# Mixing attention: biased scores and their running minimum in one VectorE instruction, from negated scaled queries

## The chip, the cores and the metric

One core of a Trainium2 chip runs the whole model: two transformer layers with a mixing sublayer each, then a recurrent layer and a stick-breaking layer. The metric is the device time of one execution in microseconds (us), less is better. Five engines work side by side, each through its own queue in order: TensorE (PE in the profile; PEld are its weight loads), VectorE (DVE), ScalarE (ACT), GpSimd (POOL) and SyncE (SP). They wait for each other through semaphores.

## The reference, cut to what matters

The change touches the two attentions of the mixing sublayer. Six heads attend in a neighbourhood (NA) with a bias table and a column mask, six in a window of 128 tokens (SWA) with a learned sink. Both also attend to 256 context tokens. Per query block:

```
s_lat = einsum(q, k_lat) * scale + bias          # SWA: no bias
s_lat = where(valid, s_lat, -1e30)
s_ctx = einsum(q, k_ctx) * scale
p = softmax(concatenate([s_lat, s_ctx]))         # SWA: the sink is one more column
o = einsum(p_lat, v_lat) + einsum(p_ctx, v_ctx)
```

## The kernel before, in words

The sublayer `mix` first projects queries, keys and values; VectorE copies the query and key tiles out of PSUM into `QK` (L1609 to L1613). Then attention runs as a list of steps (`att_steps`). A step is one pair of heads (`x` = 0, 1) and one block `t` of 128 queries. Six groups of steps (`ot` = 0 to 5: three NA, three SWA) follow each other. In layer 0 a group has six steps: four latent ones (`t` = 0 to 3, with `w` = 256, 384, 384, 256 latent keys and 256 context keys) and two that see the 256 context keys alone. In layer 1 a group has the four latent steps. So layer 0 has 36 steps, layer 1 has 24.

Every step passes through three in-order queues. The score tile `SB` has three buffers, the softmax statistics `SM` two.

- PE, for loop index `i`: `scores(i+1)` (latent matmuls L2412 into PSUM banks 0 and 1, then context matmuls L2415 into banks 2 and 3), `values(i-2)` (L2450, probabilities by values), `transposes(i-1)` (L2424). `scores` waits until banks 0 to 3 of the step before have been read.
- DVE: for step `i+1` the instruction at L1686 reads the latent scores of both heads from PSUM, multiplies by the scale, adds the bias and writes `SB`; L1690 takes the maximum over all columns of both heads; L1691 negates it. Then for step `i`: reciprocal of the row sums (L1696) and two scalings of the probabilities (L1699). At a group's end it copies the output out (L1706, L1708, L1710) and makes a low part (L1262). At an NA group's start it adds the column mask to the bias table (L1670). A sink column is copied at L1680.
- ACT: for step `i+1` a scaled copy of the context scores from PSUM to `SB` (L990); then for step `i` an exponential for each head with the row sum accumulated (L998); then for step `i-1` the copies of the transposed probabilities from PSUM (L1011, L1014); at a group's end the high part of the output (L713).

So a step's scores go PE, then DVE (latent) and ACT (context), back to DVE for the maximum, ACT for the exponentials, DVE for the scaling, PE for the transposes, ACT for the copies, PE for the values. After attention, the output projection (L2227) begins; its matmuls then fill PE without gaps. The names of semaphores that matter: `s_mm` (score matmuls done), `s_lat` (L1686 done), `s_ctx` (L990 done), `s_max` (maximum ready).

Of the kernel before, what the change touches and what calls it, by code (L numbers as in the profile page):

```python
# [21 lines left out]
P = 128  # L22
# [123 lines left out]
def build(nc, xT, ctxT, metaT, const, masks, condb, condc, modw, wu, wg, rpb, rope, four, four_c, gatew, kept, out, stop=99):  # L146
# [54 lines left out]
    MASKS = place("att_masks", [P, 7 * NA_C + 384], F32, a_t + 20480)  # L201
    RT = place("rope_tmp", [P, 2, SEQ], F32, a_t)
# [123 lines left out]
    s_lat, s_out, vf_ready, vf_rows = sem("score_bias"), sem("pv_read"), sem("v_features_ready"), sem("v_rows_mm")  # L326
# [214 lines left out]
    with nc.Block() as block:  # L541
# [155 lines left out]
        def _(act):  # L697
# [253 lines left out]
            def mix(sub, b):  # L951
# [31 lines left out]
                for i in range(-1, N + 2):  # L983
                    if i + 1 < N:
                        st, a = steps[i + 1], a0 + i + 1
                        w = st["w"]
                        act.wait_ge(s_mm, a + 1)
                        if i >= 2:
                            act.wait_ge(s_tr, tr0 + steps[i - 1]["tr0"])
                        act.activation(SB[:, a % 3, :, 1 + w:1 + w + CTX], row2(PSF[:, 2 * SEQ:4 * SEQ])[:, :, 0:CTX], ACT.Copy,  # L990
                                       scale=QSCALE).then_inc(s_ctx, 1)
                    if 0 <= i < N:
# [3 lines left out]
                        act.wait_ge(s_max, a + 1)  # L996
                        for x in range(2):
                            ins = act.activation(SB[:, a % 3, x, lo:1 + w], SB[:, a % 3, x, lo:1 + w], ACT.Exp,  # L998
                                                 bias=SM[:, a % 2, 1, x:x + 1], accum_out=SM[:, a % 2, 2, x:x + 1])
                        ins.then_inc(s_exp, 1)  # L1000
                        if st["ot"] == 1 and st["t"] == 0:
                            act.wait_ge(s_lat, 24 * mx + 4)
                            bias_load(2)
# [246 lines left out]
        def _(dve):  # L1250
# [349 lines left out]
            def mix(sub, b):  # L1600
# [3 lines left out]
                for j in range(10):  # L1604
# [3 lines left out]
                    if j < 6:  # L1608
                        ins = dve.tensor_copy(column_tiles(QK[:, j, 0:SEQ]), by_column(ps[:, 0:SEQ]))  # L1609
                        if Tj > SEQ:  # L1610
                            ins = dve.tensor_copy(QK[:, j, SEQ:T1], ps[:, SEQ:T1])
# [50 lines left out]
                for i in range(-1, N + 3):  # L1662
                    if i + 1 < N:
                        st, a = steps[i + 1], a0 + i + 1
                        sb, w, ot = SB[:, a % 3], st["w"], st["ot"]
                        if st["na"] and st["t"] == 0:
                            dve.wait_ge(tb_in[ot % 2], 16 * (mx + 1 if ot == 1 else 2 * mx + 1 + ot // 2))
                            for x in range(2):
                                tbh = TB[:, ot % 2, x].rearrange("p (n r c) -> p n r c", n=7, r=8)
                                ins = dve.tensor_tensor(tbh, tbh, MASKS[:, 0:7 * NA_C].rearrange("p (n c) -> p n c", n=7).unsqueeze(2)  # L1670
                                                        .broadcast_to([P, 7, 8, NA_C]), ALU.add)
# [4 lines left out]
                        lo = 1  # L1676
                        if st["sink"] is not None:
                            lo = 0
# [1257 lines left out]
```

## Time and profile before

| | us |
|---|---|
| median of three runs | 3761.63 (3756.4 to 3768.09) |
| span of the profiled execution, first to last instruction | 3755.4 |
| attention of layer 0 (first bias addition to first L2227) | 783.28 to 928.27: 144.99 |
| attention of layer 1 | 2253.16 to 2364.69: 111.53 |
| PE busy over the span | 3530.5 (94%) |
| DVE busy over the span | 2183.8 (58%) |
| ACT busy over the span | 1434.2 (38%) |

The profile gives no own run time of the profiled execution; its span lies 1.0 us under the fastest of the three runs and 6.2 us under their median. Busy shares over the whole span are averages over stages with different limits; PE is nearly full in the matrix stages and far less so in the two attention stages.

### The profile page before, as it was taken

How to read it: one execution, taken by the hardware profiler on the slowest of the kernel's cores; microseconds unless marked ns; L12 is line 12 of the kernel's file. 1: busy time of each engine (PE TensorE's matmuls, PEld its weight loads, DVE VectorE, ACT ScalarE, POOL GpSimd, SP SyncE). 2: the span in 40 equal slices, each digit the busy share in tenths (PEclk: the TensorE clock that was granted, in tenths of full speed). 3: DMA queues.
4: the chain of work that ended last, by engine and by line, in shares of the span. 5: the costliest groups of instructions: out<-in, count | busy, mean ns of one | idle time of the engine just before them, and what ended most of it. 6: DMA issues, size and time to landing. Idle time of an engine off the chain costs nothing.

```text
span 3755.4 us, 52062 instructions
## 1 busy us (share of the span) xinstructions
PE 3530.5 (94%) x19855; PEld 3030.4 (81%) x19855; DVE 2183.8 (58%) x3395; ACT 1434.2 (38%) x2510; POOL 721.5 (19%) x299
## 2 busy tenths in 40 slices
PE   6899999988999999999999898899998999899998
PEld 4899997856789999789999676788878898589656
DVE  6888875167488888788887429421226462541134
ACT  4433333157353333543334317432234423221353
POOL 1111112200211111211111220244442232034202
PEclk9999999999999999999999998999998999799899
DMA  6333332110233332433333220123332222022101
GB/s 227 107 124 123 124 120 86 62 36 1 91 118 116 121 117 97 157 109 116 113 113 119 82 70 17 46 90 100 96 95 68 62 79 68 1 73 90 62 1 56
DMA packets 94531, 333.55 MB, mean 89 GB/s; under 512 B 12272, under 2 KB 14576, under 8 KB 93424
## 3 DMA queue, kind: packets, MB, share of 16 engines
q1 hardware_dynamic: 91248, 316.28, 25.5%
q10 hardware_dynamic: 3072, 14.40, 1.0%
q8 instruction: 140, 2.29, 0.2%
q14 instruction: 71, 0.58, 0.0%
HBM read 322.12 MB, written 8.52 MB: 88 GB/s over the span
## 4 chain that ended last, share of the span: by engine, by line
PE 60%; issue 23%; POOL 6%; DVE 6%; ACT 3%; DMA 2%; SPq 0%; POOLq 0%; DVEq 0%; ACTq 0%
PE psum L2348 21%; PE psum L2227 14%; PE psum L2207 13%; POOL w_parts L668 6%; PE psum L2652 1%; PE psum L2668 1%; PE psum L2262 1%; PE psum L2677 1%; PE psum L2450 1%; PE psum L2121 1%; DMA mod_ring<-modw_dram 1%; PE psum L2424 1%; DVE normed L1302 1%; PE psum L2556 1%; DVE mod_products L1390 0%
## 5 line engine op out<-in xcount | busy, mean ns | idle before, releaser
L668 POOL TENSOR_TENSOR w_parts<-w_raw,w_parts 128x1024 fp32r<-128x1024 f32 x289 | 702.5, 2432 | 2929.2 <-ACT w_parts L708 2916.8
L2207 PE MATMUL psum<-h_parts,w_parts 128*128 128x264 f32 (+1 forms) x5712 | 958.2, 330 | 46.8 <-issue 11.8
L2207 PEld LDWEIGHTS psum<-h_parts,w_parts 128*128 128x128 f32 x5712 | 855.4, 191 | 144.4 <-issue 44.6
L708 ACT ACTIVATE w_parts<-w_raw 128x1024 fp32r<-128x1024 f32 x283 | 300.1, 1061 | 1123.7 <-PE psum L2207 722.5
L2227 PE MATMUL psum<-w_parts,hidden_parts 128*128 128x512 f32 x2904 | 668.3, 391 | 16.5 <-DVE hidden_parts L1262 9.6
L2227 PEld LDWEIGHTS psum<-w_parts,hidden_parts 128*128 128x128 f32 x2904 | 544.6, 188 | 135.6 <-issue 14.6
L2348 PE MATMUL psum<-h_parts,w_parts 128*128 128x384 f32 x2880 | 531.6, 336 | 16.4 <-ACT y_tok L855 14.1
L2348 PEld LDWEIGHTS psum<-h_parts,w_parts 128*128 128x128 f32 x2880 | 505.4, 189 | 20.0 <-issue 17.0
L874 ACT ACTIVATE w_parts<-psum 128x512 fp32r<-128x512 f32 x240 | 143.7, 599 | 367.9 <-PE psum L2348 147.9
L2348 PE MATMUL psum<-h_sums,w_parts 128*128 128x384 f32 x1440 | 268.9, 334 | 0.0
L2348 PEld LDWEIGHTS psum<-h_sums,w_parts 128*128 128x128 f32 x1440 | 251.3, 188 | 0.0
L1390 DVE SCALAR_TENSOR_TENSOR mod_products<-mod_ring,cond_rows 128x1024 bf16<-128x1024 f32 x128 | 180.4, 1409 | 54.4 <-DMA mod_ring<-modw_dram 51.6
L1390 DVE SCALAR_TENSOR_TENSOR mod_ring<-mod_ring,cond_rows 128x1024 f32<-128x1024 f32 x128 | 202.0, 1578 | 0.0
L1358 DVE TENSOR_TENSOR y_tok<-y_tok,psum 128x512 f32<-128x512 f32 (+1 forms) x196 | 126.7, 682 | 122.6 <-PE psum L2227 121.2
L874 ACT ACTIVATE w_parts<-w_raw_pairs 128x512 fp32r<-128x512 f32 x180 | 113.5, 631 | 220.5 <-PE psum L2348 125.4
L1543 DVE TENSOR_TENSOR w_parts<-psum,w_parts 128x512 fp32r<-128x512 f32 x240 | 164.7, 686 | 20.7 <-ACT w_parts L874 19.8
L1543 DVE TENSOR_TENSOR w_parts<-w_raw_pairs,w_parts 128x512 fp32r<-128x512 f32 x180 | 123.9, 688 | 57.6 <-ACT w_parts L874 56.6
L2348 PE MATMUL psum<-h_sum,w_parts 128*128 128x384 f32 x720 | 134.9, 335 | 0.0
L2348 PEld LDWEIGHTS psum<-h_sum,w_parts 128*128 128x128 f32 x720 | 126.4, 189 | 0.0
L2227 PE MATMUL psum<-w_parts,h_parts 128*128 128x512 f32 x480 | 109.3, 389 | 2.3 <-DVE primer L1715 2.3
L1981 DVE SCALAR_TENSOR_TENSOR sb_softplus<-psum,sb_softplus 128x512 f32<-128x512 f32 (+2 forms) x48 | 27.8, 608 | 143.6 <-ACT sb_softplus L1183 143.6
L2172 PE MATMUL psum<-h_parts,w_parts 128*128 128x256 f32 (+1 forms) x528 | 103.7, 352 | 5.8 <-DVE h_parts L1294 5.5
(352 smaller groups left out, 4121.1 us busy)
## 6 DMA issues: line engine op xcount, KB each, us to landing
w_raw<-wu_dram SPq DMA_DIRECT2D x295, 512.0 KB, 3.6
mod_ring<-modw_dram SPq DMA_DIRECT2D x128, 512.0 KB, 4.4
w_raw_pairs<-wg_dram SPq DMA_DIRECT2D x120, 512.0 KB, 3.7
kept_dram<-resid SPq DMA_DIRECT2D x2, 3136.0 KB, 9.9
resid<-kept_dram SPq DMA_DIRECT2D x16, 392.0 KB, 5.8
na_bias<-rpb_dram ACTq DMA_DIRECT2D x6, 896.0 KB, 4.7
four_dft<-four_dram ACTq DMA_DIRECT2D x2, 2048.0 KB, 8.1
mod_first_k<-modw_dram SPq DMA_DIRECT2D x7, 512.0 KB, 10.0
```

The costliest lines, as they stand in the source:

```text
L668: pool.tensor_tensor(SPL[:, s % 2, 1], RAW[:, s % 2], SPL[:, s % 2, 0].bitcast(F32), ALU.subtract).then_inc(w_split, 1)
L708: act.activation(SPL[:, u % 2, 0], RAW[:, u % 2], ACT.Copy).then_inc(w_hi, 1)
L874: act.activation(w_block(n, 0), src, ACT.Copy).then_inc(block_hi, 1)
L1302: dve.scalar_tensor_tensor(normed_tile(sub, k, a, z), XT[:, k, META + a:META + z], mod_col(l, 3 * s + 1, k, int(a >= SEQ)), PS[:, 2, SEQ * ...
L1358: return dve.tensor_tensor(y, y, bank(t), ALU.add)
L1390: return dve.scalar_tensor_tensor(dst, MODW[:, d % 2], 1.0, CBC[:, c], ALU.mult, ALU.mult, accum_out=MODS[:, t, c:c + 1])
L1543: dve.tensor_tensor(w_block(n, 1), src, w_block(n, 0).bitcast(F32), ALU.subtract)\
L2121: ins = pe.matmul(PS[0:1, 2, SEQ * hi:SEQ * hi + z - a], col("ones"), SQE[:, m, a:z], start=m == 0, stop=m == DT - 1)
L2172: ins = pe.matmul(PS[:, (u + j) % 4, a:z], SPL[:, (u + j) % 2, wp, k], H[:, xp, k, a:z], start=k == 0 and n_ == 0, stop=k == DT - 1 and n_ ...
L2207: ins = pe.matmul(PS[:, pair, PSO[a]:PSO[a] + z - a], w[:, wp, k], src[:, xp, k, t0 + a:t0 + z], start=k == 0 and n_ == 0, stop=k == KT - ...
L2227: ins = pe.matmul(bank(t), src[:, xp, k, t * P:t * P + P], SPL[:, s, wp, 4 * c:4 * c + 4].rearrange("p k m -> p (k m)"), start=k == 0 and ...
L2348: ins = pe.matmul(bank(to, HT), w_block(n, wp)[:, k], moving(m, xp)[:, k], start=m in (1, 7, 2) and k == 0 and n_ == 0, stop=k == 3 and n_ ...
```

## The change

Queries are scaled and negated once, as they are copied out of PSUM (by -QSCALE), so PSUM holds negated scaled scores. Bias and masks change sign. VectorE then reads each head's scores from PSUM with one combined instruction (tensor_tensor_reduce) that adds a second operand (a column of zeros for context scores, bias or mask for latent ones), writes the sum to `SB`, and keeps the running minimum in one column of `SM`. The minimum of the context part (or of sink and context) is the starting value of the latent part. ScalarE's exponential takes scale -1. The maximum (L1690), the negation (L1691) and ScalarE's copy of the context scores (L990) go. The context matmuls stand ahead of the latent ones, and the latent ones wait by themselves. The core of the diff:

```diff
@@ ScalarE
-                for i in range(-1, N + 2):
-                    if i + 1 < N:
-                        st, a = steps[i + 1], a0 + i + 1
-                        w = st["w"]
-                        act.wait_ge(s_mm, a + 1)
-                        if i >= 2:
-                            act.wait_ge(s_tr, tr0 + steps[i - 1]["tr0"])
-                        act.activation(SB[:, a % 3, :, 1 + w:1 + w + CTX], row2(PSF[:, 2 * SEQ:4 * SEQ])[:, :, 0:CTX], ACT.Copy,
-                                       scale=QSCALE).then_inc(s_ctx, 1)
-                    if 0 <= i < N:
+                for i in range(N + 2):
+                    if i < N:
...
-                        act.wait_ge(s_max, a + 1)
                         for x in range(2):
-                            ins = act.activation(SB[:, a % 3, x, lo:1 + w], SB[:, a % 3, x, lo:1 + w], ACT.Exp,
+                            if st["lat"]:
+                                act.wait_ge(s_max, 2 * (24 * mx + st["nlat"]) + x + 1)
+                            else:
+                                act.wait_ge(s_ctx, 2 * a + x + 1)
+                            ins = act.activation(SB[:, a % 3, x, lo:1 + w], SB[:, a % 3, x, lo:1 + w], ACT.Exp, scale=-1.0,
                                                  bias=SM[:, a % 2, 1, x:x + 1], accum_out=SM[:, a % 2, 2, x:x + 1])
@@ VectorE, copies of queries (keys stay copies)
-                        ins = dve.tensor_copy(column_tiles(QK[:, j, 0:SEQ]), by_column(ps[:, 0:SEQ]))
+                    if j < 3:
+                        ins = dve.tensor_scalar(column_tiles(QK[:, j, 0:SEQ]), by_column(ps[:, 0:SEQ]), -QSCALE, None, ALU.mult)
...
@@ VectorE, a step's scores
-                            ins = dve.tensor_copy(sb[:, :, 0:1], sink[:, :, st["sink"]:st["sink"] + 1])
-                            if not st["lat"]:
-                                step(ins)
+                            step(dve.tensor_scalar(sb[:, :, 0:1], sink[:, :, st["sink"]:st["sink"] + 1], -1.0, None, ALU.mult))
+                        for x in range(2):
+                            least = SM[:, a % 2, 0 if st["lat"] else 1, x:x + 1]
+                            first = 3.0e38 if st["sink"] is None else sb[:, x, 0:1]
+                            dve.tensor_tensor_reduce(sb[:, x, 1 + w:1 + w + CTX], bank(2 + x, CTX), ZERO.broadcast_to([P, CTX]), 1.0, first,
+                                                     ALU.add, ALU.min, least).then_inc(s_ctx, 1)
                         if st["lat"]:
-                            dve.scalar_tensor_tensor(sb[:, :, 1:1 + w], PSF[:, 0:2 * SEQ].rearrange("p (x c) -> p x c", x=2)[:, :, 0:w],
-                                                     QSCALE, bias, ALU.mult, ALU.add).then_inc(s_lat, 1)
-                            dve.wait_ge(s_lat, 24 * mx + st["nlat"] + 1)
-                        dve.wait_ge(s_ctx, a + 1)
-                        step(dve.reduce_max(SM[:, a % 2, 0, :], sb[:, :, lo:1 + w + CTX], AX_X))
-                        dve.tensor_scalar(SM[:, a % 2, 1, :], SM[:, a % 2, 0, :], -1.0, None, ALU.mult).then_inc(s_max, 1)
+                            dve.wait_ge(s_mml, 24 * mx + st["nlat"] + 1)
+                            for x in range(2):
+                                dve.wait_ge(s_ctx, 2 * a + x + 1)
+                                bias = (TB[:, ot % 2, x, st["mask"]:st["mask"] + w] if st["na"] else MASKS[:, st["mask"]:st["mask"] + w])
+                                dve.tensor_tensor_reduce(sb[:, x, 1:1 + w], bank(x, w), bias, 1.0, SM[:, a % 2, 0, x:x + 1],
+                                                         ALU.add, ALU.min, SM[:, a % 2, 1, x:x + 1]).then_inc(s_max, 1)
@@ PE, scores(i)
                     if i >= 1:
-                        pe.wait_ge(s_lat, 24 * mx + st["nlat"])
-                        pe.wait_ge(s_ctx, a)
...
+                        pe.wait_ge(s_ctx, 2 * a)
                     for x in range(2):
                         rows = slice(x * HD, x * HD + HD)
                         ins = pe.matmul(bank(2 + x, CTX), QK[rows, st["q"], t:t + P],
                                         QK[rows, st["k"], SEQ:T1], start=True, stop=True)
                     ins.then_inc(s_mm, 1)
+                    if st["lat"]:
+                        if i >= 1:
+                            pe.wait_ge(s_max, 2 * (24 * mx + st["nlat"]))
+                        k0, k1 = st["lat"]
+                        for x in range(2):
...
+                        ins.then_inc(s_mml, 1)
```

On DVE, an SWA step of layer 0 with 384 latent keys stands like this before (`const` holds the sink, `att_masks` the mask; brackets name the semaphores waited for):

```order
L1680 COPY scores<-const 128x2 [waits prob_tr,score_mm,pv_read]
L1686 SCALAR_TENSOR_TENSOR scores<-psum,att_masks 128x2x384
L1690 TENSOR_REDUCE softmax_stats<-scores 128x2 [waits score_ctx,score_bias]
L1691 TENSOR_SCALAR softmax_stats<-softmax_stats 128x2 [waits dve_step]
L1696 RECIPROCAL softmax_stats<-softmax_stats 128x2 [waits score_exp]
```

And the next such step in the changed kernel (ISA is the combined instruction; the ISA row with 128x1 is its read of the minimum):

```order
L1679 TENSOR_SCALAR scores<-const 128x2 [waits prob_tr,score_mm]
L1683 ISA scores,softmax_stats<-psum,att_masks,scores 128x256 [waits dve_step]
L1683 ISA softmax_stats 128x1
L1683 ISA scores,softmax_stats<-psum,att_masks,scores 128x256
L1683 ISA softmax_stats 128x1
L1690 ISA scores,softmax_stats<-psum,att_masks,softmax_stats 128x384 [waits score_ctx,score_lat_mm]
L1690 ISA softmax_stats 128x1
L1690 ISA scores,softmax_stats<-psum,att_masks,softmax_stats 128x384 [waits score_ctx]
L1690 ISA softmax_stats 128x1
L1696 RECIPROCAL softmax_stats<-softmax_stats 128x2 [waits score_exp]
```

Three instructions over 768, 1282 and 2 columns per partition have become four over 256, 256, 384 and 384 with a read behind each; the wait for ScalarE's copy has become a wait for the latent matmuls, and the sink's instruction is now waited for.

On ACT, in an SWA group of layer 0, before:

```order
L990 ACTIVATE scores<-psum 128x2x256 [waits prob_tr,score_mm]
L998 ACTIVATE scores,softmax_stats<-scores,softmax_stats 128x641 [waits score_max]
L998 ACTIVATE scores,softmax_stats<-scores,softmax_stats 128x641
L1011 ACTIVATE probs_t<-psum 128x512 [waits prob_tr,pv_done]
L1011 ACTIVATE probs_t<-psum 128x512 [waits prob_tr]
```

and in the changed kernel:

```order
L994 ACTIVATE scores,softmax_stats<-scores,softmax_stats 128x641 [waits score_max] x2
L1007 ACTIVATE probs_t<-psum 128x512 [waits prob_tr,pv_done]
L1007 ACTIVATE probs_t<-psum 128x512 [waits prob_tr]
L1010 ACTIVATE probs_t<-psum 128x2x128 [waits prob_tr]
L994 ACTIVATE scores,softmax_stats<-scores,softmax_stats 128x513 [waits score_max] x2
```

The copy of the next step's context scores, with its wait for PE, no longer stands ahead of this step's exponentials, and each exponential has a wait of its own.

## Rows read from the trace of the kernel before

**Rows 1.** Busy time: stretch, its length, PE, PEld, DVE, ACT, POOL, clock, DMA share, GB/s.

```profile
783.28:928.27 144.99, 115.95 (x1025) 82.53 (x1025) 118.38 (x251) 108.20 (x270) 0.00 (x0) 0.91 0.04 12
2253.16:2364.69 111.53, 91.58 (x833) 68.52 (x833) 94.41 (x179) 81.46 (x186) 0.00 (x0) 0.89 0.04 15
...
805.88:829.32 23.44, 19.36 (x174) 13.84 (x172) 20.55 (x41) 17.94 (x46) 0.00 (x0) 0.93 0.13 41
876.87:899.82 22.95, 19.39 (x174) 14.16 (x176) 19.12 (x44) 18.05 (x45) 0.00 (x0) 0.93 0.01 1
2270.33:2288.13 17.80, 15.30 (x140) 11.79 (x140) 16.62 (x30) 13.38 (x31) 0.00 (x0) 0.90 0.16 52
2322.91:2339.10 16.19, 13.89 (x144) 10.46 (x142) 14.91 (x32) 13.39 (x32) 0.00 (x0) 1.00 0.01 2
```

**Rows 2.** Timeline of DVE, an NA group of layer 1: start, us, engine, line.

```profile
2272.45 0.69 DVE L1686 SCALAR_TENSOR_TENSOR scores<-psum,na_bias 128x512 f32<-128x512 f32 x1
...
2274.51 0.16 DVE L1696 RECIPROCAL softmax_stats<-softmax_stats 128x2 f32<-128x2 f32 x1
...
2275.50 0.95 DVE L1686 SCALAR_TENSOR_TENSOR scores<-psum,na_bias 128x768 f32<-128x768 f32 x1
...
2278.08 0.16 DVE L1696 RECIPROCAL softmax_stats<-softmax_stats 128x2 f32<-128x2 f32 x1
...
2284.85 1.22 DVE L1690 TENSOR_REDUCE softmax_stats<-scores 128x2 f32<-128x1024 f32 x1 [0.57 <-ACT scores L990]
```

**Rows 3.** Timeline of one SWA group of layer 1: PE, DVE and ACT.

```profile
2322.44 1.31 PE L2450 MATMUL psum<-probs_t,v_tok 128*64 128x128 f32 x20 [0.74 <-ACT probs_t L1014]
...
2326.32 0.17 DVE L1680 COPY scores<-const 128x2 f32<-128x2 f32 x1 [0.21 <-PE psum L2415]
...
2329.97 0.16 DVE L1680 COPY scores<-const 128x2 f32<-128x2 f32 x1
...
2333.76 0.68 DVE L1708 COPY to_split<-psum 128x512 f32<-128x512 f32 x1
2334.50 1.09 PE L2450 MATMUL psum<-probs_t,v_tok 128*64 128x128 f32 x16 [1.56 <-DVE to_split L1708]
...
2335.14 0.58 ACT L990 ACTIVATE scores<-psum 128x512 f32<-128x512 f32 x1
...
2335.61 0.82 ACT L998 ACTIVATE scores<-scores,softmax_stats 128x641 f32<-128x641 f32 x1
...
2338.63 1.31 PE L2450 MATMUL psum<-probs_t,v_tok 128*64 128x128 f32 x20 [0.74 <-ACT probs_t L1014]
```

**Rows 4.** Three DVE instructions: busy us and mean ns, or ns least/median/most.

```profile
L1710 DVE COPY to_split<-psum 128x256 f32<-128x256 f32 x6 | 2.5, 418 | 2.7 <-PE psum L2450 2.7
...
L1302 DVE SCALAR_TENSOR_TENSOR to_split<-resid,mods,psum x48: 473/481/748, 601.5 to 2440.1; 128x256 f32<-128x256 f32 x32, 128x512 f32<-128x512 f32 x16
...
L1790 DVE TENSOR_TENSOR_SCAN lru_x<-gate_decay,gate_i x8: 1257/1257/1259, 2896.4 to 2936.8; 128x528 f32<-128x528 f32 x8
```

**Rows 5.** Timeline of DVE, an instruction with an accumulated sum, and its successors.

```profile
69.02 1.22 DVE L1390 SCALAR_TENSOR_TENSOR mod_products<-mod_ring,cond_rows 128x1024 bf16<-128x1024 f32 x1
70.17 0.08 DVE L1390 DVE_READ_ACCUMULATOR mod_products<-mod_ring,cond_rows 128x1 f32 x1
70.17 3.42 DVE L1390 SCALAR_TENSOR_TENSOR mod_ring<-mod_ring,cond_rows 128x1024 f32<-128x1024 f32 x1
```

**Rows 6.** Line L1609 (query and key copies): ns, and idle us before them, times.

```profile
L1609 DVE COPY qk<-psum x12: 681/692/694, 623.5 to 2152.2; 128x512 f32<-128x512 f32 x12
...
  PE psum L2207: 66.8, 8
```

**Rows 7.** Waits in an NA group of layer 0: us in total, times, longest.

```profile
DVE softmax_stats L1690 <- ACT scores L990: 1.7, 3, 0.8
```

**Rows 8.** Chain of waits, shares by line, an SWA group of layer 0.

```profile
by line: PE psum L2450 21.8%; PE psum L2424 19.1%; PE psum L2412 10.1%; PE psum L2415 8.7%; DVE scores L1699 6.7%; DVE softmax_stats L1690 6.5%; ACT scores L998 5.9%; ACT scores L990 5.3%; DVE scores L1686 3.8%; issue 3.0%; ACT probs_t L101
```

**Rows 9.** Timeline of PE after the attention of layer 1.

```profile
2364.69 43.77 PE L2227 MATMUL psum<-w_parts,h_parts 128*128 128x512 f32 x192 [1.23 <-DVE primer L1715]
```

More of the change, by code:

```diff
@@ L1607, in mix @@
                     ps = PS[:, (u + j) % 4, 0:Tj]
-                    if j < 6:
-                        ins = dve.tensor_copy(column_tiles(QK[:, j, 0:SEQ]), by_column(ps[:, 0:SEQ]))
+                    if j < 3:
+                        ins = dve.tensor_scalar(column_tiles(QK[:, j, 0:SEQ]), by_column(ps[:, 0:SEQ]), -QSCALE, None, ALU.mult)
                         if Tj > SEQ:
-                            ins = dve.tensor_copy(QK[:, j, SEQ:T1], ps[:, SEQ:T1])
+                            ins = dve.tensor_scalar(QK[:, j, SEQ:T1], ps[:, SEQ:T1], -QSCALE, None, ALU.mult)
+                    elif j < 6:
+                        dve.tensor_copy(column_tiles(QK[:, j, 0:SEQ]), by_column(ps[:, 0:SEQ]))
+                        ins = dve.tensor_copy(QK[:, j, SEQ:T1], ps[:, SEQ:T1])
+                    elif j < 9:
+                        ins = dve.tensor_scalar(QK[:, j, 0:Tj], ps, -QSCALE, None, ALU.mult)
                     else:
@@ L2402, in scores @@
                     st, a = steps[i], a0 + i
+                    t = st["t"] * P
                     if i >= 1:
-                        pe.wait_ge(s_lat, 24 * mx + st["nlat"])
-                        pe.wait_ge(s_ctx, a)
-                    t = st["t"] * P
-                    if st["lat"]:
-                        k0, k1 = st["lat"]
-                        for x in range(2):
-                            rows = slice(x * HD, x * HD + HD)
-                            pe.matmul(bank(x, k1 - k0), QK[rows, st["q"], t:t + P], QK[rows, st["k"], k0:k1], start=True, stop=True)
+                        pe.wait_ge(s_ctx, 2 * a)
                     for x in range(2):
@@ L2417, in scores @@
                     ins.then_inc(s_mm, 1)
+                    if st["lat"]:
[3 more added lines that the diff above has]
+                        for x in range(2):
+                            rows = slice(x * HD, x * HD + HD)
+                            ins = pe.matmul(bank(x, k1 - k0), QK[rows, st["q"], t:t + P], QK[rows, st["k"], k0:k1], start=True, stop=True)
+                        ins.then_inc(s_mml, 1)
                 def transposes(i):
@@ L2464, in mix @@
                 pe.wait_ge(s_trc, tr0 + steps[-1]["tr0"] + steps[-1]["tr"])
-                pe.wait_ge(s_ctx, a0 + N)
-                pe.wait_ge(s_lat, 24 * mx + 24)
+                pe.wait_ge(s_ctx, 2 * (a0 + N))
+                pe.wait_ge(s_max, 2 * (24 * mx + 24))
                 last_out_units(sub, u + 16, H, DT, [(v_ready, e + 6)] * 3, e, cap=6)
@@ L2796, in attention_masks @@
         ws = np.clip(qc - 8, 0, GRID_W - 16)
-        m[:, n * NA_C:(n + 1) * NA_C] = np.where((kc >= ws) & (kc < ws + 16), 0.0, NEG)
+        m[:, n * NA_C:(n + 1) * NA_C] = np.where((kc >= ws) & (kc < ws + 16), 0.0, -NEG)
     rel = np.arange(384)[None, :] - P - p[:, None]
-    m[:, 7 * NA_C:] = np.where(np.abs(rel) <= 128, 0.0, NEG)
+    m[:, 7 * NA_C:] = np.where(np.abs(rel) <= 128, 0.0, -NEG)
     return m
```

13 lines of the change are left out of this document (5 added, 8 removed).

## The prediction, made before the changed kernel ran

> **What bounds the kernel now.** I read first where the changed lines run. The table of busy time by stretch shows two windows, 145.0 us in layer 0 and 111.5 us in layer 1 [rows 1]; outside them the change touches only the query copies. In both windows no engine is full: DVE is busy 82 and 85% of the time, PE 80 and 82%, ACT 75 and 73%. So the stage is not bound by one engine but by a loop through several queues, and what matters is which piece of it lies on the loop. When the loop ends, PE starts the output projection and runs 192 matmuls in 43.8 us with no gap [rows 9], so what attention gains is not given back there.
>
> Then I read one group of each kind. An NA group of layer 1 takes 17.80 us with 16.62 us of DVE work [rows 1]: DVE itself is the loop, and its largest stall is 0.57 us, where the maximum waits for ScalarE's copy of the context scores [rows 2]. An SWA group of layer 1 takes 16.19 us from one L2450 at 2322.44 to its counterpart at 2338.63, and its loop can be read off end to end [rows 3]: PE from 2322.44 to 2326.32 (3.88: values, transposes, next scores), two DVE steps to 2329.97 and 2333.76 (3.65 and 3.79), output copy, marker and ScalarE's high part to 2335.14 (1.38), ScalarE's context copy to 2335.61 (0.47), then exponentials and probability copies to 2338.63 (3.02). The sum is 16.19. The groups of layer 0 have two context-only steps more. In NA they are led by DVE much as in layer 1 (20.55 of 23.44 us) [rows 1], with 1.7 us of DVE stalls for the context copy [rows 7]; in SWA the four PE lines make up 60% of the chain of waits, the context copy 5.3% and the score lines L1690 and L1686 together 10.3% [rows 8].
>
> **The change, part by part.**
>
> *The combined instruction* does not occur in the trace as such. Its nearest rows: a 256-wide copy from PSUM, 418 ns, and a two-source instruction that also fetches a scalar per partition and reads PSUM, 481 ns at 256 wide [rows 4]. Widths cost 0.26 us per 256 columns (0.95 against 0.69 us) [rows 2], so 384 wide with a fetched starting value comes to 0.48 + 0.13 = 0.61 us. An instruction with an accumulated sum is followed by a read of 0.08 us, and the next instruction starts with that read, 0.07 us before the first one's recorded end [rows 5]. So I count 0.35 us for a context part in NA (a constant as start), 0.41 in SWA (start fetched from the sink column), 0.41 and 0.54 for latent parts of 256 and 384, and nothing for the reads except some 0.1 us before a consumer may go on.
>
> The Trainium skill (VectorE: DVE Perf Modes, Rules for kernel authors) says that instruction count is to be kept low since fixed costs return with each. By it alone, counting a 0.16 us instruction such as the reciprocal [rows 2] for each of the five that come on top (three become eight), a step would lose 0.8 us and the gain below would vanish. The trace prices the four reads otherwise, as they begin with their successors [rows 5].
>
> *One latent step on DVE.* Before, from the bias instruction to the reciprocal: 2.06 us at 256 (2272.45 to 2274.51) and 2.58 us at 384 (2275.50 to 2278.08) [rows 2]. After, in NA: 2 x 0.35 + 2 x 0.41 = 1.52 and 2 x 0.35 + 2 x 0.54 = 1.78, so -0.54 and -0.80. In SWA the starts are fetched and the sink's instruction (0.17 us [rows 3], now waited for, so about 0.24 instead of 0.07) goes ahead: 0.17 + 4 x 0.41 = 1.81 and 0.17 + 2 x 0.41 + 2 x 0.54 = 2.07, so -0.25 and -0.51. A context-only step changes by 0.1 us at most; its maximum and negation take about as long as two context parts.
>
> *ScalarE's context copy* (0.58 us [rows 3], 60 times) goes. Where DVE stalls for it, the stall goes; where it stands ahead of the exponentials on the loop, 0.47 us go [rows 3].
>
> *PE's score matmuls* are the same in number and kind; the context ones come first and may start when DVE has read the two context banks, the latent ones when both latent parts are read. Before, latent banks came free with the end of L1686, 0.69 or 0.95 us after its start; after, 1.5 to 1.8 us after the start of DVE's score work. Queued behind a late latent matmul on PE are values and transposes of earlier steps. That is a new risk, priced below.
>
> *Query copies* become multiplications by a constant, same shapes, also from PSUM. I count nothing: DVE idles 66.8 us before eight of the twelve 512-wide copies, waiting for PE [rows 6]. If that cover were gone, the bound is 0.06 us each (481 against 418 ns [rows 4]) for 15 instructions, 1 us. The bias addition has the same shapes; the exponential's scale of -1 is a constant.
>
> **The sum.** NA, layer 1: DVE is the loop: -0.54 - 0.80 - 0.80 - 0.54 and the 0.57 us stall, -3.25 at most. PE is busy 15.30 of 17.80 us [rows 1], which leaves it 2.5; I take -2.8, part of the overlap in PE's records being slack. SWA, layer 1: two 384-key steps on the loop, -1.02, and the context copy, -0.47, so -1.5, from 16.19 to 14.7; PE's two waits of 0.74 and 1.56 us [rows 3] put its own work at 13.9, which is below that. NA, layer 0: -2.68 for the four steps, -0.2 for the context-only ones, and up to -1.7 for stalls [rows 7] would be -4.6, but PE is busy 19.36 of 23.44 us [rows 1], and I take -3.2. SWA, layer 0: the context copy's 5.3% of 22.95 us is 1.2, one 384-key step 0.51: -1.7. Three groups of each: -8.4 - 4.5 - 9.6 - 5.1 = -27.6. At the end of each layer's last group the context copy stands once or twice more on the way out: -1 each, -2. Together -29.6, taken as **-30 us**: span 3755.4 to 3725, and the median 3761.6 to **3732 us** (the median lies 6.2 above the profiled span, and I carry that over).
>
> **Bounds of this case.** If every combined instruction is 0.1 us dearer (120 context and 96 latent, 21.6 us of DVE work, two thirds of it on the loops), 14 us come back: 3746. If everything in the NA sums that I held back for PE comes (3 x 0.45 + 3 x 1.4 = 5.6) and PE's idle stretches shorten so that its clock, granted at 0.89 to 0.93 in three of the four groups and at 1.00 in the fourth [rows 1], comes up by some 4% of 208 us of PE work, 14 us more go: 3718. So 3718 to 3746.
>
> **The rivals.**
>
> *Half rate (slower).* The scan, the row's other instruction with a running value, takes 1257 ns for 528 columns [rows 4], about twice the time per column of the bias instruction [rows 2]. If the running minimum works at that pace, a 256-wide part takes 0.62 to 0.68 us and a 384-wide one 0.94: 2.6 and 3.12 us a latent step against 2.06 and 2.58, +0.54 each, and +0.44 for a context-only step. NA groups: 4 x 0.54 - 0.57 = +1.6 in layer 1 and 4 x 0.54 + 0.9 - 1.7 = +1.4 in layer 0; SWA: +1.0 and +0.3. Three of each is +13: 3775. Between -30 at full rate and +13 at half rate the turn lies at some 0.7 of the extra 0.26 us per 256 columns. Against it: the accumulated sum runs 1024 columns in 1.22 us [rows 5], the full rate.
>
> The Trainium skill (Vector Engine (DVE) Microarchitecture Reference, Points that are easy to get wrong) has a rule of this kind: a two-source form whose sources are both 4-byte SBUF data runs at half rate, since no port is left for the accumulator. The row of 1.22 us has two such sources and disagrees [rows 5]; by that rule the time would be this rival's.
>
> *PE waits for the latent banks (no change).* The latent matmuls may wait until 1.5 to 1.8 us into DVE's score work instead of 0.7 to 0.95. If each of the 48 latent steps loses 0.4 us of PE's time on the loop, 19 of the 30 us come back: 3751, within the bound. Against it: PE has 2.6 us of values and transposes between two score sets, and the 20 matmuls at 2322.44 alone last 1.31 us [rows 3].
>
> *More than forecast.* ScalarE loses 60 x 0.58 = 35 us of work and each exponential may start after its own head's minimum. If the group loops fall to PE's bare work at full clock (13.9 us in an SWA group of layer 1), the sum is about -44: 3718.
>
> **How the numbers follow.** Forecast 0.66, half rate 0.12, PE waits 0.10, more 0.12. Changes within 0.3% (11.3 us) can hardly be told from none. Faster: the forecast and the larger gain, and 0.01 of the waits: 0.79. Same: 0.09. Slower: 0.12. The range runs from 3715 to 3756: it takes in the forecast's bounds, the larger gain and the PE rival, and leaves out half rate (0.12) and a little below.
>
> **What would show each step.** The profile after should have no L990, L1690 and L1691 of before, context parts of about 0.42 to 0.48 us, latent parts of 0.48 and 0.61, an NA group of layer 1 near 15.0 us and an SWA group near 14.7, the attentions near 130 and 98 us, and DVE's busy time in them down by 12 to 14 us each. The forecast is wrong if the combined rows are 0.6 us or longer, if PE's latent matmuls wait for the minimum for 0.4 us and more in most steps, or if a group's length falls by less than half of what DVE's work falls.

## The result, and the profile after

The changed kernel takes 3729.66 us (median of 4 runs, 3722.76 to 3733.22), the kernel before beside it 3763.26 (4 runs). The ratio is 0.9913, with a 95% interval of 0.9896 to 0.9929. The forecast was 3732 for the median, 2.3 us off; the gain is 33.6 us where 30 were forecast. The profiled execution spans 3730.7 us, 5.7 more than the 3725 forecast for it: outside the two attentions it took 3507.9 us, where the profile of the kernel before took 3498.9. How the gain comes about did not come out as I had written it, and that is what the experiments below are for.

First the busy time by stretch of the kernel after: the stretch, its length, PE, PEld, DVE, ACT, POOL, clock, DMA share, GB/s. The lines answer to those of [rows 1]: the attention of layer 0, then one NA and one SWA group in it, then the same for layer 1. An NA group runs from its bias addition to the next one, an SWA group from its first sink line to the first of the next.

```profile
786.57:913.71 127.14, 109.11 (x1024) 75.50 (x1025) 105.34 (x395) 89.39 (x234) 0.00 (x0) 0.97 0.04 13
...
804.98:825.13 20.15, 17.98 (x174) 12.56 (x173) 17.78 (x66) 14.91 (x39) 0.00 (x0) 1.00 0.14 47
866.96:887.31 20.35, 18.11 (x175) 12.55 (x172) 17.52 (x69) 14.92 (x41) 0.00 (x0) 1.00 0.00 1
2240.83:2336.52 95.69, 85.03 (x833) 62.51 (x833) 82.30 (x299) 68.80 (x162) 0.00 (x0) 0.96 0.05 18
...
2253.93:2269.32 15.39, 14.99 (x152) 10.87 (x152) 14.25 (x51) 12.12 (x30) 0.00 (x0) 1.00 0.21 62
2299.34:2313.74 14.40, 13.90 (x144) 10.47 (x142) 13.29 (x53) 11.44 (x29) 0.00 (x0) 1.00 0.01 2
```

The attentions are 17.85 and 15.84 us shorter, 33.7 together. DVE's busy time falls by 13.0 and 12.1 us, ACT's by 18.8 and 12.7. PE does the same matmuls and still shows 6.8 and 6.6 us less, at a clock that is now full in all four groups shown. The SWA group of layer 1 is 14.40 us long with 13.90 of PE work, so little is left there beside what PE itself needs. Against what I had named beforehand: attentions near 130 and 98 us (127.1 and 95.7), an NA group of layer 1 near 15.0 (15.39), an SWA group near 14.7 (14.40), DVE 12 to 14 us less in each.

The new instructions appear as a custom DVE operation, the reads of their result as rows of their own. The durations of all 216 (least, median and most, in ns):

```profile
L1683 DVE CUSTOM_DVE_ANT_0 scores<-psum,att_masks x60: 418/422/428, 788.7 to 2281.3; 128x256 f32<-128x256 f32 x60
L1683 DVE CUSTOM_DVE_ANT_0 scores<-psum,att_masks,scores x60: 480/485/489, 846.8 to 2324.7; 128x256 f32<-128x256 f32 x60
L1690 DVE CUSTOM_DVE_ANT_0 scores<-psum,na_bias,softmax_stats x48: 479/548/621, 789.4 to 2282.0; 128x256 f32<-128x256 f32 x24, 128x384 f32<-128x384 f32 x24
L1690 DVE CUSTOM_DVE_ANT_0 scores<-psum,att_masks,softmax_stats x48: 478/546/621, 847.6 to 2325.5; 128x256 f32<-128x256 f32 x24, 128x384 f32<-128x384 f32 x24
```

And one NA step of 256 keys with the start of a step of 384, on DVE's timeline (layer 1), which answers to [rows 2]:

```profile
2256.05 0.43 DVE L1683 CUSTOM_DVE_ANT_0 scores<-psum,att_masks 128x256 f32<-128x256 f32 x1
2256.40 0.08 DVE L1683 DVE_READ_ACCUMULATOR2_ANT softmax_stats<- 128x1 f32 x1
2256.40 0.42 DVE L1683 CUSTOM_DVE_ANT_0 scores<-psum,att_masks 128x256 f32<-128x256 f32 x1
2256.74 0.08 DVE L1683 DVE_READ_ACCUMULATOR2_ANT softmax_stats<- 128x1 f32 x1
2256.74 0.48 DVE L1690 CUSTOM_DVE_ANT_0 scores<-psum,na_bias,softmax_stats 128x256 f32<-128x256 f32 x1
...
2257.55 0.16 DVE L1696 RECIPROCAL softmax_stats<-softmax_stats 128x2 f32<-128x2 f32 x1
...
2259.23 0.62 DVE L1690 CUSTOM_DVE_ANT_0 scores<-psum,na_bias,softmax_stats 128x384 f32<-128x384 f32 x1
2259.77 0.09 DVE L1690 DVE_READ_ACCUMULATOR2_ANT softmax_stats<- 128x1 f32 x1
2259.77 0.62 DVE L1690 CUSTOM_DVE_ANT_0 scores<-psum,na_bias,softmax_stats 128x384 f32<-128x384 f32 x1
```

Read the starts, not the durations: 2256.05, 2256.40, 2256.74 is a pitch (from one start to the next) of 0.35 us for a context part, and 2259.23 to 2259.77 one of 0.54 for a latent part of 384. Each read starts together with the next instruction. From the first part to the reciprocal the step takes 1.50 us; I had 1.52.

### The profile page after: what moved, and what is told of

It is laid out like the page before. It is cut to its first block, busy times and chain, and to the rows that moved or that the text cites. A ratio compares the mean times of both kernels' runs of the same rounds, so it can differ in the third digit from the quotient of the medians.

```text
span 3730.7 us, 52148 instructions
## 1 busy us (share of the span) xinstructions
PE 3522.9 (94%) x19855; PEld 3022.9 (81%) x19855; DVE 2158.1 (58%) x3659; ACT 1403.3 (38%) x2450; POOL 723.4 (19%) x299
## 3 DMA queue, kind: packets, MB, share of 16 engines
q10 hardware_dynamic: 3072, 14.40, 1.0%
## 4 chain that ended last, share of the span: by engine, by line
PE 60%; issue 23%; POOL 6%; DVE 6%; ACT 2%; DMA 2%; SPq 0%; POOLq 0%; DVEq 0%; ACTq 0%
PE psum L2348 22%; PE psum L2227 14%; PE psum L2207 13%; POOL w_parts L669 6%; PE psum L2654 1%; PE psum L2670 1%; PE psum L2452 1%; PE psum L2262 1%; DMA mod_ring<-modw_dram 1%; PE psum L2679 1%; PE psum L2121 1%; DVE normed L1298 1%; PE psum L2558 1%; PE psum L2426 1%; DVE mod_ring L1386 1%
## 5 line engine op out<-in xcount | busy, mean ns | idle before, releaser
L2227 PEld LDWEIGHTS psum<-w_parts,h_parts 128*128 128x128 f32 x480 | 91.1, 190 | 21.8 <-issue 2.7
```

The costliest lines, as they stand in the source:

```text
L2227: ins = pe.matmul(bank(t), src[:, xp, k, t * P:t * P + P], SPL[:, s, wp, 4 * c:4 * c + 4].rearrange("p k m -> p (k m)"), start=k == 0 and ...
```

## The experiments

All the readings below are of the two attentions, from the first bias line (DVE) to the first matmul of the output projection (PE). Each is one profiled execution. The attention of the changed kernel, profiled again unedited, came back to 0.01 us in each layer, that of the kernel before only to 2.2 us in sum (its clock differed, see below). The rest of the program, which no experiment edits, scattered between 3498 and 3514 us over the 14 profiles. Medians therefore carry several us that are not of the edit. "vs before" is the ratio to the kernel before with its 95% interval; four kernels were run once.

| kernel | layer 0 | layer 1 | sum | median | vs before |
|---|---|---|---|---|---|
| before | 144.99 | 111.53 | 256.52 | 3763.26 | |
| after | 127.14 | 95.69 | 222.83 | 3729.66 | 0.9913 (0.9896 to 0.9929) |
| e0_control | 127.15 | 95.68 | 222.83 | 3727.75 | 0.9910 (0.9893 to 0.9926) |
| e1_act_copy | 131.89 | 101.70 | 233.59 | 3748.73 | 0.9958 (0.9942 to 0.9975) |
| e2_latent_first | 135.61 | 103.75 | 239.36 | 3747.27 | 0.9961 (0.9947 to 0.9975) |
| e3_dve_long | 136.10 | 103.20 | 239.30 | 3749.27 | 0.9965 (0.9950 to 0.9981) |
| b1_context_first | 142.35 | 107.47 | 249.82 | 3754.84 | 0.9993 (0.9983 to 1.0002) |
| e9_latent_first_both | 127.79 | 96.02 | 223.81 | 3729.91 | 0.9920 (0.9903 to 0.9936) |
| e10_copy_and_order | 141.56 | 108.65 | 250.21 | 3755.07 | 0.9987 (0.9976 to 0.9998) |
| e4_joint_wait | 129.34 | 95.67 | 225.01 | 3727.64, one run | |
| b0_before_again | 144.84 | 109.47 | 254.31 | 3762.55, one run | |
| e11_vector_relief | 129.05 | 96.74 | 225.79 | 3732.40, one run | |
| e7_transposes_first | 126.46 | 94.77 | 221.23 | 3728.28, one run | |
| e8_all | 125.59 | 94.53 | 220.12 | 3727.74 | 0.9909 (0.9893 to 0.9926) |

My theory (A) was that VectorE's shorter score work is the larger part of the gain; the rivals were that it is ScalarE's copy, gone from ahead of the exponentials (B), and that the new order of the score matmuls plays no part (C).

**The control.**

> The changed kernel once more, nothing edited. Every theory: attention 127 us in layer 0 and 96 us in layer 1, each within 1 us. The first pair of profiles differed by 9 us the other way outside attention, where the change only scales the queries. If that is the change's doing, the stretch outside attention is again 3508 us within 2; if it is scatter between executions, it moves by several us while the attentions stay.

Its attentions are the same to 0.01 us; outside them it took 3725.9 - 222.8 = 3503.1 us, where the first profile had 3507.9. What differs outside attention is scatter between executions. The scaled query copies cost nothing that can be seen: before the change a copy of 768 columns takes 958 ns, and the multiplication in its place 957 (layer 0, before and after):

```profile
L1613 DVE COPY qk<-psum 128x768 f32<-128x768 f32 x4 | 3.8, 958 | 29.4 <-PE psum L2207 29.4
```

```profile
L1612 DVE TENSOR_SCALAR qk<-psum 128x768 f32<-128x768 f32 x3 | 2.9, 957 | 22.0 <-PE psum L2207 22.0
```

**ScalarE's copy put back.** PE waits for it as before the change; VectorE waits ahead of the latent parts, as it had waited ahead of the maximum. The edit, in part:

```
+ act.wait_ge(s_mm, a0 + i + 2)
+ act.activation(SPARE[:], K[:, 0:2 * CTX]..., ACT.Copy, scale=QSCALE).then_inc(s_x, 1)   # ahead of the exponentials
+ dve.wait_ge(s_x, a + 1)        # ahead of the latent parts
+ pe.wait_ge(s_x, a)             # ahead of the next context matmuls
```

> ScalarE's context copy is put back in its place: 60 copies of 512 columns (from constants to a place that nobody reads; the scores are left as they are), with the waits of before, of VectorE and of PE's next scores on it. Theory A (VectorE's shorter score work is the larger part of the 33.7 us that the two attentions gained; ScalarE's relief the smaller): 6 to 12 us come back, layer 0 near 133 and layer 1 near 100. Theory B (the copy in front of the exponentials was the larger part): 20 us or more come back.

10.8 us came back (60 copies of 629 ns, 37.7 us of work, most of it beside other engines; before the change their median was 600 ns, so the stand-in is a little dearer). By the attentions this is A's side, and B fell. But the median rose by 21 us over the control's, which would be B's side. In the profile the rest of that lies outside attention (3514.3 us there, the longest of all), and 3.5 us of it ahead of the first attention, where no edited instruction has yet run (790.29 against 786.75). It is taken for scatter; that is argued from one profile.

**The old order of the score matmuls.** The edit, shortened:

```
+ pe.wait_ge(s_max, 2 * (24 * mx + st["nlat"]))
  pe.wait_ge(s_ctx, 2 * a)
+ latent matmuls
  context matmuls
- pe.wait_ge(s_max, ...)
- latent matmuls
```

> PE does the latent score matmuls first and the context ones after them, as before the change, and waits for both kinds of minimum at the start; VectorE and ScalarE are as in the changed kernel. Theory A: VectorE's first context part starts later by a pair of latent matmuls (0.6 to 0.9 us) in each of 48 steps, of which PE's cover of values and transposes hides a part: 8 to 13 us come back, layer 0 near 133, layer 1 near 101. Theory C (the order is of no weight, the two kinds were only renamed): within 2 us of the changed kernel. The rival of the prediction (PE's wait for the latent banks in the new order costs as much as the early context parts bring): a few us faster than the changed kernel.

16.5 us came back, more than A had expected and as much as in the next run, which takes back VectorE's shortening. Theory C fell. The waits of PE's weight loads (us in total, times, longest) show where; of this kernel in layer 0 and layer 1:

```profile
PEld psum L2412 <- DVE softmax_stats L1690: 24.2, 18, 7.7
...
PEld psum L2412 <- DVE softmax_stats L1690: 16.8, 16, 7.7
```

and of the changed kernel, the same wait of the latent matmuls (there L2418):

```profile
PEld psum L2418 <- DVE softmax_stats L1690: 6.2, 13, 1.1
...
PEld psum L2418 <- DVE softmax_stats L1690: 2.9, 5, 1.1
```

These do not compare as they stand: at the start of each attention PE waits for VectorE's first scores, and with the new order that wait (6.9 and 6.7 us) falls on the context matmuls, which come first:

```profile
PEld psum L2409 <- DVE softmax_stats L1683: 8.1, 5, 6.9
...
PEld psum L2409 <- DVE softmax_stats L1683: 8.9, 4, 6.7
```

With the old order PE stands 41 us for VectorE's minima, with the new one 26 us in all. VectorE in turn waits 24.9 us for PE's scores with the old order (its lines L1679 and L1683) and 10.4 with the new one (L1690 as well). Each engine waits some 15 us longer for the other, near the 16.5 us that came back: with the old order they take turns where they had overlapped.

**VectorE's score work as long as before.** The line that is added, shortened:

```
+ dve.reduce_max(SPARE[:, ...], K[:, 0:2 * n]..., AX_X)   # between context and latent parts; n by width
```

> VectorE's score work of a latent step is made as long as it was before: between the context and latent parts stands an idle reduction of 0.54 and 0.80 us (NA, 256 and 384 keys) or 0.25 and 0.51 us (SWA), whose result nobody reads; ScalarE and PE are as in the changed kernel. Theory A: 17 to 22 us come back (24 x 0.67 + 24 x 0.38 us of work, some 25 us, four fifths of it on the loops), layer 0 near 138 and layer 1 near 105. Theory B: less than 10 us come back, since the work would lie beside ScalarE's and PE's.

The busy time of its two attentions:

```profile
787.83:923.93 136.10, 111.00 (x1024) 75.44 (x1025) 117.31 (x419) 90.20 (x234) 0.00 (x0) 0.97 0.04 13
...
2249.84:2353.04 103.20, 87.06 (x832) 62.91 (x833) 93.79 (x323) 69.03 (x162) 0.00 (x0) 0.95 0.05 16
```

DVE's busy time rose by 12.0 and 11.5 us, to within 1.1 us of what it was before the change; 16.5 of these 23.5 us came back in the end. That is just below A's range and far above B's: 70% of the added work lies on the loops. Not all of it need be VectorE's own time. The idle reduction stands ahead of the latent parts and frees the latent banks later as well, and PE's weight loads of the latent matmuls wait 18.9 us for that minimum, against 9.1 in the changed kernel. The run does not tell the two apart.

**The order alone, on the kernel before.** The edit, shortened:

```
+ pe.wait_ge(s_ctx, a);  context matmuls
+ pe.wait_ge(s_lat, ...);  latent matmuls .then_inc(s_mml, 1)
+ dve.wait_ge(s_mml, ...)        # ahead of the bias instruction
```

> The kernel before, with one part of the change alone: PE does the context score matmuls first, behind the wait for ScalarE's copy, then the latent ones behind the wait for the bias instruction, and VectorE's bias instruction waits for a signal of its own. After the run with the old order (16.5 us back) two theories stand. Order by itself (an earlier context matmul is a gain of its own): 8 us or more come off before's 256.5 us of attention. Order as a partner of the combined instruction (before, latent banks came free early, 0.7 to 1.0 us into the score work; the combined instruction frees them only at its end, so with the old order PE has to stand still, and the new order only averts that): within 2 us of 256.5.

249.8 us is 6.7 less than before, between the two expectations. But part of it is the clock: layer 1 ran at 0.97 in this profile, at 0.89 in the first one of before, and at 0.93 when the kernel before was profiled once more (below). Against that second profile 4.5 us are left, and the ratio of the medians, 0.9993, does not tell this kernel from before. So the order by itself brings a few us at most.

**Latent first on both engines.** The edit, in words and in part:

```
  pe:  latent matmuls behind s_max, then context matmuls behind s_ctx
  dve: latent parts first (start: sink or 3.0e38), then context parts (start: the latent minimum)
  act: wait_ge(s_ctx, 2 * a + x + 1)
```

> The changed kernel with latent scores first on PE and on VectorE too: latent matmuls behind the wait for the latent parts, which now come first on VectorE, then context matmuls behind the context parts, which now carry the last minimum. Order as a partner (each kind of bank is freed in the order in which it is filled again): 223 to 226 us of attention, as in the changed kernel. Order by itself (context scores must come early): about 239, as with the old order on PE alone.

223.8 us, within 1.0 us of the changed kernel. It is not that context scores must come early: PE must refill the banks in the order in which VectorE empties them. e2_latent_first broke that, and lost 16.5 us. It did two things at once: PE could refill nothing until VectorE had read everything, and what VectorE reads first came last. No run takes these two apart.

**Copy and order back, the combined instruction kept.** The edits of e1_act_copy and e2_latent_first, in one kernel.

> The two edits e1_act_copy and e2_latent_first together: of the change only the combined instruction and its negated scales are left. If the parts added up, attention would take 222.8 + 10.8 + 16.5 = 250 us, 6.4 less than before. If VectorE's shorter work were the gain by itself (theory A taken strictly), it would stay near 240. If copy and order hide behind each other, 240 to 245.

The busy time of its two attentions:

```profile
787.22:928.78 141.56, 109.05 (x1024) 77.06 (x1025) 107.74 (x395) 108.84 (x270) 0.00 (x0) 0.96 0.04 12
...
2256.50:2365.15 108.65, 86.79 (x833) 63.85 (x833) 84.44 (x299) 82.06 (x186) 0.00 (x0) 0.94 0.04 15
```

250.2 us: the parts add up to 0.1 us. DVE has 10 us less to do in each attention than before, and yet the combined instruction without the other two edits is worth 6.3 of the 33.7 us (4.1 against the second profile of before, below). Theory A in its strict form fell: how much VectorE's shorter work is worth depends on the other two edits.

**One wait for both heads.** The edit, shortened:

```
+ act.wait_ge(s_max, 2 * (24 * mx + st["nlat"]) + 2)     # ahead of both exponentials; s_ctx likewise
- act.wait_ge(s_max, 2 * (24 * mx + st["nlat"]) + x + 1)
```

> Both exponentials of a step wait for both heads' minima, as before the change. If each head's own minimum lets its exponential start early (by 0.4 to 0.5 us on the loop of 60 steps), several us come back; if ScalarE takes the first exponential later anyway or VectorE is held elsewhere, within 1 us of 222.8.

Layer 1 is the same (95.67 against 95.69). Layer 0 is 2.2 us longer, but there the clock came back later at the start of attention (0.72 against 1.00 in the second sixteenth of the stretch), so this run does not tell what the wait costs; it is no large part.

**Before, once more.**

> The kernel before once more, unedited, since its two attentions were profiled at a granted clock of 0.91 and 0.89 and every kernel after at 0.94 or more, and since the new order alone showed 249.8 us at 0.93 and 0.97. If the low clock belongs to the kernel's pattern of work, 145 and 111.5 us come again within 1 us, and what the new order alone gained (6.7 us) is its own. If the clock is an accident of the execution, the attentions come out shorter, towards 142 and 108, and the order alone gained little.

Layer 0 came again to 0.15 us, with its low clock (0.92). Layer 1 was 2.1 us shorter at 0.93. So most of the low clock belongs to the kernel before, and some 2 of the 33.7 us to the execution that was profiled.

**Less work on VectorE.** The edit, in part:

```
+ pool.tensor_tensor(tbh, MASKS..., tbh, ALU.subtract)   # groups 1 and 2; DVE waits for s_tb
+ dve.tensor_scalar(col("sink", 0, 12), ..., -1.0, None, ALU.mult)   # once
- step(dve.tensor_scalar(sb[:, :, 0:1], sink..., -1.0, None, ALU.mult))
+ dve.tensor_copy(sb[:, :, 0:1], sink...);  first = col("sink", l * 6 + 3 * x + st["sink"], 1)
```

> The changed kernel with less on VectorE: the mask addition to the bias tables of the second and third NA group moves to GpSimd, which stands idle there, and the sinks are negated once, so that the step's copy of them needs no wait. If VectorE's work is still on the loops: 2 x 2.09 us per layer and 0.1 to 0.15 us for each of 30 SWA steps, half to all of it, so 4 to 11 us off 222.8. If PE and ScalarE now bound the groups, or GpSimd slows VectorE down while both work: within 2 us.

DVE's busy time fell by 3.0 and 2.5 us, and yet the attentions grew by 3.0, outside both expectations. The timeline of all engines in layer 0 (start, us, engine, line) shows why:

```profile
811.89 4.34 POOL L693 TENSOR_TENSOR na_bias<-att_masks,na_bias 128x896 f32<-128x896 f32 x2 [20.10 <-DMA na_bias<-rpb_dram]
...
813.00 3.59 DVE L1716 TENSOR_SCALAR scores<-scores,softmax_stats 128x640 f32<-128x640 f32 x2
...
816.97 1.97 PE L2469 MATMUL psum<-probs_t,v_tok 128*64 128x128 f32 x16 [3.19 <-DVE to_split L1727]
...
818.88 2.40 PE L2443 MATMUL psum<-const,scores 128*128 128x128 f32 x10
```

A pair of scalings that takes 1.02 us at 819.78 takes 3.59 us while GpSimd works, and ends 0.36 us after GpSimd does (816.59 and 816.23). Each of the two scalings ends 0.35 us behind one of GpSimd's two additions. A combined instruction, which reads its scores from PSUM, kept its 0.61 us beside it (812.27). Behind the pair the output copy is late and PE stands 3.19 us. In that pause its clock falls: it is granted 0.52 from 816 to 818 and 0.50 from 818 to 822, and ten transposes take 2.40 us in place of 1.31. It happens once per layer (3.30 us in layer 1). The Trainium skill (SBUF — State Buffer, Who interferes with whom) says that VectorE and GpSimd share a pair of SBUF ports, that an SBUF-to-SBUF scaling can take it, and that the one that comes second stands still for the whole of the other's instruction. The rows agree.

**Transposes ahead of values, and all together.** The edit of the first:

```
+ if 0 <= i - 1 < N: transposes(i - 1)
  if i >= 2: values(i - 2)
- if 0 <= i - 1 < N: transposes(i - 1)
```

> The changed kernel with PE's transposes of a step ahead of the values of the step before it. The largest wait of the profile after is ScalarE's probability copy for PE's transposes (25.5 and 16.8 us). If that wait is on the loops: 2 us or more off 222.8. If the values, which come later by as much, hold up the next copies instead (these wait for the values): within 1 us, or slower.

> The edits of e11_vector_relief and e7_transposes_first in one kernel. If both gains come and add up: 5 to 10 us off the changed kernel, near 3720 us. If the groups are at PE's own work by then (85 to 109 us busy in the two attentions): 3 us or less.

221.2 us for the one, 220.1 for all: 1.6 and 2.7 us off, between the expectations of the first and within the smaller one of the second, in which GpSimd still holds VectorE up once in each layer (3.66 us at 816.37, 2.94 at 2260.14). The median of e8_all, 3727.74, cannot be told from that of the changed kernel.

## Why the prediction was right, and which steps were not

- *The combined instruction* was priced to 0.02 us: 0.42, 0.48 and 0.62 us in the rows above, 0.42, 0.48 and 0.61 predicted; pitches 0.35 and 0.54 as predicted. In SWA, steps of 256 and 384 keys take 1.81 and 2.09 us (2299.34 to 2301.15 and 2302.15 to 2304.24), 1.81 and 2.07 predicted. Half rate is refuted by the same rows. The rule on two SBUF sources that the prediction set beside this rival would not have reached the combined instruction, which reads its scores from PSUM. The row of 3.42 us in [rows 5] does not speak for half rate either: all 128 instructions of that form have a median of 1.22 us, and this one ran beside an addition on GpSimd that began at 69.61. The Trainium skill (DVE: opcode table, instruction layouts, handler registers and perf-mode slots; Datapath and trigger behaviour) names a reason: a running value that a stage takes from its own last result costs nothing, while the scan sends its value back to an earlier stage and runs at half throughput. The trace has both, the scan of [rows 4] at 2.4 ns a column and the minimum at (0.54 - 0.35) us for 128 more columns and one scalar fetch, some 1.0 ns (0.06 us taken off for the fetch, 481 against 418 ns [rows 4]). Which way the minimum takes inside the engine no run shows, only its pace.
- *The group sums* were all a little small. Three NA groups of layer 0: -10.9 us (predicted -9.6); three SWA groups with their tail: -7.0 (-6.1); in layer 1 -9.1 (-8.4) and -6.7 (-5.5). The NA group of layer 1 that the prediction read gained less than forecast (17.80 to 15.39, -2.4 for -2.8); the first group of that layer made up for it (17.17 to 13.10, -4.1). The rows for the four stretches, before and after:

```profile
783.28:854.19 70.91, 57.02 (x478) 40.05 (x480) 59.16 (x114) 51.78 (x127) 0.00 (x0) 0.86 0.07 23
854.19:928.27 74.08, 58.94 (x549) 42.47 (x549) 59.22 (x138) 56.42 (x144) 0.00 (x0) 0.95 0.01 1
2253.16:2306.37 53.21, 43.79 (x348) 31.82 (x350) 47.81 (x81) 37.00 (x83) 0.00 (x0) 0.80 0.08 30
2306.37:2364.69 58.32, 47.80 (x487) 36.70 (x487) 46.60 (x98) 44.45 (x103) 0.00 (x0) 0.97 0.01 1
```

```profile
786.57:846.62 60.05, 51.89 (x475) 35.97 (x476) 50.93 (x186) 41.92 (x109) 0.00 (x0) 0.94 0.08 27
846.62:913.71 67.09, 57.21 (x552) 39.53 (x549) 54.42 (x210) 47.47 (x127) 0.00 (x0) 1.00 0.00 1
2240.83:2284.94 44.11, 38.91 (x354) 27.32 (x356) 40.52 (x141) 30.83 (x73) 0.00 (x0) 0.92 0.11 37
2284.94:2336.52 51.58, 46.12 (x483) 35.19 (x479) 41.78 (x159) 37.97 (x91) 0.00 (x0) 1.00 0.01 1
```

- *ScalarE's context copy* stood in the sum at 3 x 0.57 + 3 x 0.47 + 3 x 1.2 + 2 = 8.7 us and some of the stalls in layer 0's NA groups; putting it back cost 10.8. *VectorE's shorter work* is the rest of the sum, some 21 us; making it as long again cost 16.5. One term was too small, the other too large, and the order and the clock had none. That the total came within 4 us of what the attentions gained, and the median within 2.3, is in part luck.
- *"PE's score matmuls are the same in number and kind"* is where the account fell short. I priced the order as a risk only, the rival in which PE, with the new order, waits for the latent banks and 19 us come back. With the new order that wait came to 9.1 us, 18 times in 48 steps, so the rival did not come. A wait of this kind is real, and e2_latent_first shows it at 16.5 us; but it is what the combined instruction would cost with the *old* order, and the reordering in the same change is what removes it. I had taken cause and cure for one risk. The three parts, each taken out alone, are worth 10.8 (copy), 16.5 (order) and 16.5 (VectorE's time), 43.8 together where the change brought 33.7; the instruction alone is worth 6.3.
- *The clock* stood in the bound and not in the sum. Before, at the end of an NA group PE waited for the output copy behind DVE's long maximum, and its clock fell after the pause. The timeline of the kernel before (PE), and the windows beside it:

```profile
2283.52 1.09 PE L2450 MATMUL psum<-probs_t,v_tok 128*64 128x128 f32 x16 [2.30 <-DVE to_split L1706]
2284.55 2.33 PE L2424 MATMUL psum<-const,scores 128*128 128x128 f32 x10
```

```profile
2282.00:2284.00 2.00, 0.48 (x8) 0.48 (x10) 1.93 (x5) 0.37 (x1) 0.00 (x0) 1.00 0.00 0
2284.00:2286.00 2.00, 2.00 (x19) 1.83 (x16) 1.43 (x2) 2.00 (x5) 0.00 (x0) 0.67 0.03 8
2286.00:2288.00 2.00, 2.00 (x11) 1.50 (x11) 1.81 (x6) 1.60 (x5) 0.00 (x0) 0.50 0.00 0
```

  The same place after (PE): there is no pause, and ten transposes take 1.31.

```profile
2265.19 1.09 PE L2452 MATMUL psum<-probs_t,v_tok 128*64 128x128 f32 x16
2266.22 1.31 PE L2426 MATMUL psum<-const,scores 128*128 128x128 f32 x10
```

  What a fall of the clock costs can be read in part. The kernel before was profiled twice, and some groups ran at a different clock each time. The third NA group and the last SWA group with its tail, both of layer 1, in the first profile and in the second:

```profile
2288.13:2306.37 18.24, 15.94 (x146) 11.87 (x146) 16.69 (x30) 13.53 (x31) 0.00 (x0) 0.91 0.00 1
2339.10:2364.69 25.59, 19.66 (x203) 15.42 (x199) 16.78 (x37) 17.16 (x40) 0.00 (x0) 0.93 0.01 1
```

```profile
2291.41:2309.20 17.79, 14.71 (x152) 10.94 (x150) 16.61 (x31) 13.91 (x33) 0.00 (x0) 1.00 0.00 1
2341.58:2366.17 24.59, 18.35 (x202) 14.26 (x199) 16.79 (x37) 17.06 (x40) 0.00 (x0) 1.00 0.01 1
```

  A fall of the clock goes with 0.45 and 1.00 us here, and with 0.29, 0.19 and 0.13 in the three groups of layer 0 that differ in the same way. Of the 4 us by which the attentions gained more than the sum, 2.2 are the first profile's own: against the second one (254.31) they gained 31.5. The rest stays open. e10_copy_and_order has the full clock outside the first eighth of each attention and still takes 250.2 us, so the 27.4 us between it and the changed kernel do not come from falls inside the attentions. No run changed the clock alone.

## What to carry to other kernels

When one instruction takes the place of two, ask when it gives back its buffers, not only how long it lasts: here the shorter instruction freed the latent banks later, and 16.5 of the 33.7 us would have been lost without a second edit that refills the banks in the order in which they come free. A change of several parts is best read with each part taken out alone and with one part kept alone; the two differ by as much as the parts lean on each other. And an engine that looks idle (GpSimd here) is free help only if its work does not hold up the engine that it is to relieve.

## What the runs showed of the hardware that was not expected

- The read of an accumulated result (0.08 us) starts together with the next instruction in 194 of the 216 cases of the kernel after, so it adds nothing to the pitch there. Behind the other 22 there is a gap, mostly a wait for PE or ScalarE.
- VectorE's SBUF-to-SBUF scaling stood still while GpSimd's two-input addition ran (3.59, 3.30, 3.66 and 2.94 us for a pair that takes 1.02), while its instructions that read PSUM beside it did not.
- PE's clock fell to half (1.2 in place of 2.4 GHz) in two places looked at closely: after a pause of 2.30 us, during the work that followed it (1.00 from 2282 to 2284, 0.67 from 2284 to 2286), and in a pause of 3.19 us itself (0.52 from 816 to 818). It came back at about 2288 and 823 us. A pause of 0.24 us in the kernel after (2268.83) and one of 1.56 us in the kernel before (2334.50 [rows 3]) brought no fall: the clock stands at 1.00 from 2268 to 2270 and from 2332 to 2338. Both attentions begin at half clock in all 14 profiles (0.50 to 0.59 in the first sixteenth), while PE stands for VectorE's first scores (6.5 us in layer 0 of the kernel after).
